# One program in two transformer blocks: a ring of twelve expert tiles, the routing block merged with the norm before it, and the output stored from the loop's block

## What is computed

```
# recurrence, per head: a 64x64 state S, one step per token
S = S * w_t + (S z_t) b_t^T + v_t k_t^T;  y_t = S r_t

# end of layer 1
xl = xl + g1 * mix_l                                # projection and residual
h  = rmsnorm(xl, norm2_g) * (1 + sc2) + sh2         # 256 tokens x 1024
logits = h @ router                                 # 256 x 8
top_logit, top_e = top_k(logits, 2); gates = softmax(top_logit)
y[t] = sum over the 2 chosen e: gates * (silu(h @ w_gate[e]) * (h @ w_up[e])) @ w_down[e]   # hidden width 3584
xl = xl + g2 * y
out = rmsnorm(xl, final_g)
```

## Time and profile before

| What | Value |
|---|---|
| Median of three runs | 3042.98 us |
| The profiled execution, its own time | 3046.43 us |
| Its span | 3044.6 us |
| Mean granted TensorE clock | 0.962 |
| PE busy | 2809.3 us (92%) |
| DVE, ACT, POOL busy | 964.3, 438.5, 175.5 us |
| First expert tile on PE | 2010.8 us |
| Expert weights, 8 items of 44 MB | 352 of the 557 MB read |

### The profile page before, as it was taken

How to read it: one execution, slowest core, us unless ns; L and a number is a source line. 1 busy time by engine, 2 the same in 40 slices (tenths; PEclk the granted TensorE clock), 3 DMA queues, 4 the chain that set the end, 5 groups by cost and what they waited for, 6 DMA issues and landing times. The chain is left out here.

```text
span 3044.6 us, 54863 instructions
## 1 busy us (share of the span) xinstructions
PE 2809.3 (92%) x24263; PEld 1632.7 (54%) x24263; DVE 964.3 (32%) x1936; ACT 438.5 (14%) x980; POOL 175.5 (6%) x210
## 2 busy tenths in 40 slices
PE   8999998699889799999979979789999999999998
PEld 6678986444478564444444457645344453434534
DVE  2422586538654326640025654320000000000001
ACT  1401100213332110000023141200000000000001
POOL 0000000000134000000000034000000000000000
PEclk9999999899999899999989989889999999999999
DMA  7234577221300125532222120069999899999995
GB/s 237 97 129 146 190 249 246 90 97 60 83 4 3 56 83 193 202 116 76 76 74 83 71 44 3 11 273 367 341 347 365 329 350 344 348 366 338 349 339 212
DMA packets 181989, 562.28 MB, mean 185 GB/s; under 512 B 28752, under 2 KB 41420, under 8 KB 165370
## 3 DMA queue, kind: packets, MB, share of 16 engines
q1 hardware_dynamic: 160675, 497.73, 45.6%
q0 software_dynamic: 13856, 53.11, 4.9%
q10 hardware_dynamic: 7223, 7.85, 0.9%
HBM read 557.43 MB, written 1.23 MB: 183 GB/s over the span
## 5 line engine op out<-in xcount | busy, mean ns | idle before, releaser
L1279 PE MATMUL bank<-normed,weight_ring 128*128 128x256 f32 (+2 forms) x2528 | 668.1, 425 | 12.7 <-PEq L2165 7.9
L1279 PEld LDWEIGHTS bank<-normed,weight_ring 128*128 128x128 f32 x2528 | 456.6, 192 | 220.7 <-issue 181.4
L2637 PE MATMUL bank<-weight_ring,work 128*32 128x384 f32 (+1 forms) x3072 | 310.7, 560 | 36.0 <-issue 34.8
L680 PE MATMUL bank<-normed,weight_ring 128*128 128x512 f32 (+1 forms) x704 | 281.6, 561 | 24.7 <-PEq L1377 24.7
L2637 PE MATMUL bank<-work 128*32 128x384 f32 (+1 forms) x3072 | 298.0, 540 | 0.0
L1279 PE MATMUL bank<-work,weight_ring 128*128 128x256 f32 (+2 forms) x928 | 282.1, 462 | 4.3 <-PEq L1247 4.3
L229 DVE SCALAR_TENSOR_TENSOR work<-work,small 128x512 f32<-128x512 f32 x336 | 237.7, 749 | 28.4 <-DMA work<-in_mod_w 21.9
L1279 PEld LDWEIGHTS bank<-work,weight_ring 128*128 128x128 f32 x928 | 174.8, 191 | 107.8 <-issue 94.2
L2637 PEld LDWEIGHTS bank<-weight_ring,work 128*32 128x32 f32 x3072 | 100.5, 113 | 235.1 <-issue 235.1
L680 PEld LDWEIGHTS bank<-normed,weight_ring 128*128 128x128 f32 x704 | 135.5, 194 | 169.7 <-issue 165.4
L2637 PEld LDWEIGHTS bank<-work 128*32 128x32 f32 x3072 | 97.4, 110 | 183.6 <-issue 183.6
(11 more groups left out here) (347 smaller groups left out, 2423.4 us busy)
## 6 DMA issues: line engine op xcount, KB each, us to landing
weight_ring<-in_moe_w_down SPq DMA_DIRECT2D x64, 1024.0 KB, 10.4
work<-in_mod_w POOLq DMA_DIRECT2D x48, 1024.0 KB, 6.1
work<-in_moe_w_down SPq DMA_DIRECT2D x48, 1024.0 KB, 10.9
weight_ring<-in_w_in SPq DMA_DIRECT2D x36, 1024.0 KB, 5.4
weight_ring<-in_moe_w_gate SPq DMA_DIRECT2D x32, 1024.0 KB, 5.5
work<-in_moe_w_gate SPq DMA_DIRECT2D x32, 1024.0 KB, 8.5
weight_ring<-in_moe_w_up SPq DMA_DIRECT2D x32, 1024.0 KB, 5.3
work<-in_moe_w_up SPq DMA_DIRECT2D x32, 1024.0 KB, 6.4
```

Source lines behind the costliest of these rows:

```text
L680: last = self.nc.tensor.matmul(self.bank(t)[:, 0:a.shape[-1]], tile[:, j * P:(j + 1) * P], a, start=k == 0, stop=k == DT - 1)
L1279: last = nc.tensor.matmul(banks(gi)[j][:, to], w[:, k, j * P:(j + 1) * P], a, start=k0 + k == 0, stop=k0 + k == total - 1)
L2637: last = nc.tensor.matmul(self.bank[3 * up + a][g * R:(g + 1) * R, 0:n], xg[:, k, a * R:(a + 1) * R], w[:, g * n:(g + 1) * n], start=k == ...
```

## The change

It has five parts.

- **Recurrence.** The product with the identity goes. The first of the two other products starts the sum. DVE now adds the old state to the sum from PSUM, in place, and then multiplies by the decay: two additions and two products instead of two products.
- **Ring of 12.** Eight slots in `work`. The first four k tiles of down come singly, in 0.5 MB tiles, so an item has 48 tiles, four turns of 12. A slot of the next item waits for the tile twelve before it.
- **Routing.** The loads go onto ACT's queue at the start of the last projection. The second half of the norm leaves that block and stands in the routing block. There PE turns the rows of token tile 0, sums the squares, computes the logits of tile 0, then those of tile 1 feature by feature behind the norm. DVE makes each tile's choice when its logits are there. The gates come behind the list of items. The first gather stands in this block as well. SP starts the first twelve tiles at its beginning, always those of expert 0; item 0 is always one of expert 0. POOL clears the buffers.
- **Residual.** DVE adds gate column times scattered rows from PSUM to the residual, eight operations of 128x256 in place of four additions of 128x512; `acc` goes, and so do the eight operations behind the loop.
- **End.** The store stands in the loop's block. The last scatter is in two halves in different banks, each followed by its own four operations on DVE; PE turns pieces of the residual as they are done; ACT loads the table of the root before the squares.

Some semaphores now share a name with others, to make room for the new ones; that adds no instruction. Cut to its core, the diff is below. Its places are, in order: the constant; `scan_pe`; `scan_dve`; `block_two` in layer 1; the routing block in `experts`; DVE in the loop's block; and PE, ACT and DVE behind the loop.

```diff
-EXPERT_SLOTS = 8
+EXPERT_SLOTS = 12
...
-            for d in range(2):
-                nc.tensor.matmul(S[d][:, 0:2 * P], self.pr.tab("ident"), self.state[:, 2 * d:2 * d + 2].rearrange("p f n -> p (f n)"),
-                                 start=True, stop=False)
-                    nc.tensor.matmul(S[d][:, fc], btok[r, 2 * d + 1, fc], self.vtok[r, tile[d], fc], start=False, stop=False)
+                    nc.tensor.matmul(S[d][:, fc], btok[r, 2 * d + 1, fc], self.vtok[r, tile[d], fc], start=f == 0, stop=False)
...
             dve.wait_ge(self.ssum.sem, self.ssum.at(n + 1))
+            for d in range(2):
+                both = self.state[:, 2 * d:2 * d + 2]
+                nc.vector.tensor_tensor(both, S[d][:, 0:2 * P].rearrange("p (f n) -> p f n", f=2), both, ALU.add).then_inc(self.carried.sem, 1)
             dve.wait_ge(self.dready.sem, self.dready.at(n + 1))
             for d in range(2):
-                last = nc.vector.tensor_tensor(self.state[:, 2 * d:2 * d + 2], S[d][:, 0:2 * P].rearrange("p (f n) -> p f n", f=2),
-                                               self.decay[:, c, 2 * d:2 * d + 2], ALU.mult)
+                both = self.state[:, 2 * d:2 * d + 2]
+                dve.wait_ge(self.carried.sem, self.carried.at(2 * n + d + 1))
+                last = nc.vector.tensor_tensor(both, both, self.decay[:, c, 2 * d:2 * d + 2], ALU.mult)
...
-                self.linear(groups, tail=norms[1])
+                final_gain = ar.take("final_gain", D)
+                route_tables, loads = self.route_loads()
+                self.linear(groups, loads=[(final_gain, bass.AP(ins["final_g_2"].tensor, 0, [[0, P], [1, D]]))] + loads)
                 ar.free("cvout")
-                final_gain = ar.take("final_gain", D)
-                self.experts(gates(1)[0][1], final_gain)
-        self.store(final_gain)
+                self.experts(gates(1)[0][1], norms[1], final_gain, *route_tables)
...
+            @block.sync
+            def _(sync):
+                for j in range(EXPERT_SLOTS):
+                    sync.dma_start(place(j), source(j, 0)).then_inc(full[j].sem, 16)
+            @block.gpsimd
+            def _(pool):
+                nc.gpsimd.memset(y[:, 1:A], 0.0).then_inc(ymoved.sem, A)
+                nc.gpsimd.memset(y[:, 0], 0.0).then_inc(added.sem, 1)
+                nc.gpsimd.memset(spread, 0.0).then_inc(gmoved.sem, 1)
             @block.tensor
             def _(pe):
+                turn_rows(0)
+                norm.add_up(pe, self.bank[3])
                 for t in range(2):
                     for k in range(DT):
+                        if t == 1:
+                            norm.wait_scaled(pe, k)
                         last = nc.tensor.matmul(self.bank[t][:, 0:E], hT[:, k, SEQ + t * P:SEQ + (t + 1) * P], router[:, k, :], start=k == 0, stop=k == DT - 1)
                     last.then_inc(logits.sem, 1)
+                turn_rows(1)
+                pe.wait_ge(choices.sem, choices.at(2))
...
+                pe.wait_ge(rowsm.sem, rowsm.at(1))
+                pe.wait_ge(picked.sem, picked.at(1))
+                gather()
             @block.scalar
             def _(act):
+                norm.square(act, lambda eng, k: None)
+                move_rows(0)
+                norm.root_and_shift(act)
+                nc.scalar.activation(gt[:, 0, 80:81], self.tab("ones")[:, 0:1], ACT.Exp)
+                move_rows(1).then_inc(rowsm.sem, 1)
 ...
+                act.wait_ge(gathered.sem, gathered.at(1))
+                move_gathered()
...
-                def add_scattered():
-                    for g in range(4):
-                        part = acc[:, 2 * g:2 * g + 2].rearrange("p k t -> p (k t)")
-                        last = nc.vector.tensor_tensor(part, self.bank[3 + g], part, ALU.add)
-                    last.then_inc(added.sem, 1)
+                def add_scattered(k, apart=False):
+                    part = self.bank[scatter_bank(k % 2, k // 2, apart)][:, (k % 2) * SEQ:(k % 2 + 1) * SEQ]
+                    return nc.vector.scalar_tensor_tensor(xT[:, k, LAT], part, gate_column(k), xT[:, k, LAT], ALU.mult, ALU.add)
...
-                scatter()
+                scatter(apart=True)
+                for k in range(DT):
+                    pe.wait_ge(added.sem, n_items + added.at(1 + max(4, k // 2 + 4 * (k % 2) + 1)))
+                    for t in range(2):
+                        last = nc.tensor.transpose(self.bank[3 + 2 * t + k // 4][:, (k % 4) * P:(k % 4 + 1) * P],
+                                                   xT[:, k, SEQ + t * P:SEQ + (t + 1) * P], ident)
+                nc.scalar.activation(stat[:, 0, 6:7], self.tab("ones")[:, 0:1], ACT.Sqrt)
+                for i, (b, t) in enumerate(((0, 0), (0, 1), (1, 0), (1, 1))):
+                    act.wait_ge(rows.sem, rows.at(i + 1))
+                    nc.scalar.activation(dump[:, 2 * t + b], self.bank[3 + 2 * t + b], ACT.Square, accum_out=stat[:, t, b:b + 1]).then_inc(squared.sem, 1)
+                for i in range(2):
+                    dve.wait_ge(scattered.sem, n_items + scattered.at(i + 1))
+                    for g in range(4):
+                        add_scattered(2 * g + i, apart=True).then_inc(added.sem, 1)
```

More of the change, by code:

```diff
@@ new lines, in experts @@
+        starts = (0, 4 * GROUP)
+        n_in, n_single = 4 * DT, 4
+        down = [(k, 1) for k in range(n_single)] + [(k, 2) for k in range(n_single, D_FFE // P, 2)]
+        per = n_in + len(down)
+        assert per % EXPERT_SLOTS == 0
+        width = 4 * GROUP
+        more = ar.take("more_slots", EXPERT_SLOTS - WEIGHT_SLOTS, width)
+        slots = [self.ring[:, i].rearrange("p k n -> p (k n)") for i in range(WEIGHT_SLOTS)] + [more[:, i] for i in range(EXPERT_SLOTS - WEIGHT_SLOTS)]
+        for i, q in enumerate(self.slot_full):
+            q.advance(16 * len(self.weights[i::WEIGHT_SLOTS]))
@@ new lines, in experts, with source @@
+        full = self.slot_full + [self.counted(f"side_load{i}_landed") for i in range(EXPERT_SLOTS - WEIGHT_SLOTS)]
+        turns = per // EXPERT_SLOTS
+        used = self.tile_used
+        wg, wu, wd = (ins[f"moe_w_{n}_2"][0] for n in ("gate", "up", "down"))
+        def source(j, e):
+            if j < n_in:
+                part, k = divmod(j, DT)
+                w, (c, n) = (wg, wu)[part % 2], (starts[part // 2], 4 * widths[part // 2])
+                return w.rearrange("e r c -> (e r) c")[bass.ds(e * D + k * P, P), c:c + n]
+            rows = wd.rearrange("e r c -> (e r) c")
+            k, n = down[j - n_in]
+            return rows[bass.ds(e * D_FFE + k * P, n * P), :].rearrange("(k p) n -> p k n", p=P)
@@ L2516, in experts @@
-        pick = ar.take("pick", 2, ITEM_TOKENS)
         gated = ar.take("gated", 2, A, P)
-        spread = ar.take("spread", A, SEQ)
-        widths = (GROUP, (D_FFE - 4 * GROUP) // 4)
-        starts = (0, 4 * GROUP)
-        n_in, n_down = 4 * DT, D_FFE // (2 * P)
-        per = n_in + n_down
-        width = 4 * GROUP
-        more = ar.take("more_slots", EXPERT_SLOTS - WEIGHT_SLOTS, width)
-        slots = [self.ring[:, i].rearrange("p k n -> p (k n)") for i in range(WEIGHT_SLOTS)] + [more[:, i] for i in range(EXPERT_SLOTS - WEIGHT_SLOTS)]
```

299 lines of the change are left out of this document (129 added, 170 removed).

## The result

The changed kernel takes 3006.71 us (median of 4 runs, 3004.55 to 3008.84). The kernel before took 3042.4 beside it (4 runs, 3039.94 to 3046.82). The ratio is 0.988, with a 95% interval of 0.9866 to 0.9894: 35.7 us less. Forecast were 3014 and a range of 3003 to 3027.

The account below looks back on a forecast made before the run. PE's own matrix work was taken to bound the loop, leaving way in, way out and recurrence: -18.5-6-4.8=-29.3 from the median 3042.98 gives 3013.7, predicted as 3014, range 3003 to 3027.

Parts of the forecast that it names:

- Ring, 0: Expert tile ring of 12: no gain, as PE was not seen to wait for any tile; 0 us.
- Way in, -18.5: Last residual to first expert tile: shorter chain, gather hidden beside DVE's list; 18.5 us less, bounds 12 to 25.5.
- the slow first tile: Loop entry: some 3 us of PE idle behind the gather slow the first tiles; 2.6 us added to the way in.
- PE doesn't catch up: First expert tiles: twelve issued early at 3 us a tile, nine there at the first tile, so PE never waits.
- Way out, -6: Last scatter's start to last scaling: the scaling starts 6.2 us earlier, counted as 6 us less; bounds 4 and 7.5.
- Recurrence, -4.8: Recurrence's 16 chunks: identity product goes, DVE gets additions; 4.8 us less, bounds -17 and +12.
- Loop, +0: Loop over items: eight DVE operations for four behind the scatter are covered, 0; without that cover 0.8 us an item.
- The edge was weights: Rival, edges between items: the ring takes perhaps 3 us off each of 7 edges, 2993 us; chance 0.06.
- Overlap pays less: Rival: instruction fetch competes with 12 MB of tiles, routing stays slow; 18 us gain in all, 3025; chance 0.15.
- Port lock: Rival, recurrence: DVE's decay product loses 0.96 us per chunk to a port shared with POOL; 3029 us; chance 0.06.
- Deeper queue, slower edge: Rival, jumps back: more tiles queue before the instruction fetch; doubled edges give +40, 3054 us; chance 0.04.
- An extra item: Rival, item list: forcing item 0 to expert 0 adds an item of 127 us, 3141, if without tokens; chance 0.01.

Follow-up runs that it names:

- both edges: Changed kernel with eight slots instead of twelve: 3006.81 us with the loop as it was, 2968.32 us with PE's back edge announced.
- the announced loop: Changed kernel with one more instruction on PE at the loop's head that announces the target of the jump back: 2967.03 us.
- -8.8 alone: Kernel before with only the recurrence's two edits, no product with the identity and two additions on DVE: 3033.11 us, ratio 0.9973.
- free queues: Changed kernel with the first twelve expert tiles started in the loop's block, after the item count is read: 3012.04 us, 5.3 more.
- before with the announcement: Kernel before with nothing but the back edge of PE's loop announced: 3014.0 us, ratio 0.9905.

## Why the prediction was right, point by point

- **Ring, 0.** Right, shown with both edges (3006.81 for 3006.71; 2968.32 for 2967.03). That the edge was the jump back and not weights is shown by the announced loop. The landing times of the tiles grew: the median of the gate tiles in `weight_ring` was 5.5 us before, 11.7 in the changed kernel with eight slots and 16.0 with twelve. With twelve more of them are under way at once, and PE waits for none of them.
- **Way in, -18.5.** It was -22.6, and +1.4 for the slow first tile: -21.2. The bounds (12 to 25.5) hold it. The chain was as described, with the gather level with DVE's list. Wrong was the logits' clock: 3.5 for each half was taken from a stretch at 0.50, though the 10 us of idle PE that had lowered it were one of the things that the change removes. The halves took 1.85 and 2.43, and the second follows ACT's shift (2.45), so 1.9 of those 7.0 us were gained and not 3.5. The entry took 1.8 behind DVE's end and not 2.5. The slow first tiles cost 1.4 and not 2.6, but this was one execution: in four others with such an entry they cost 2.9 (8.2 to 8.3 us), so the term was sound and its miss is luck. The first expert tile was forecast near 1985 and came at 1973.05; of the 12 us, 4.6 lie ahead of the first recurrence, 4.8 in the recurrence, 0.9 between and 1.6 here. (The 4.6 of gain that the prediction puts ahead of that tile should be 4.8 by its own term.) The first tile was forecast with the twelve loads running early, but their price (5.3) stood nowhere in the sum: "PE doesn't catch up" was right, and the early start was what it rested on.
- **Way out, -6.** It was -7.4, at the edge of the bounds (7.5). The same error: the 4.4 from the first transpose to the end of the squares was a time at the half clock. A square itself takes 0.60 in both kernels, but before, each waited for PE's transposes, and they followed each other every 0.85; now it is every 0.58, and the 4.4 became 3.6. Another 0.4 is that the scaling of token tile 0 starts before the root of tile 1 is taken. No drain shows behind the load of the table.
- **Recurrence, -4.8.** It was -9.6 in the profile and -8.8 alone: the term that was mis-sized most. The step that failed is "I take 0.30 for all 16". The reasoning for the one chain holds within the last step alone (-0.39 for -0.30; two additions move the decay by 0.67 and not by 0.76). Nowhere else is it 0.30: across to the last step it is -1.0, within a step -1.15, and across to a new step it lies between -0.1 and +0.8. The prediction named both ways of hiding, PE's time behind POOL and ACT and DVE's time behind an idle DVE, but put their difference at the same 0.30 without a row. And the row that it gave for DVE, the 1.52 before line 598, is not the wait that hides the additions; that is the 0.79 behind it.
- **Loop, +0.** Its edges and first tiles grew by 1.8 us over seven edges (34.8 to 35.8 in waits, 51.8 to 52.6 in the 48 instructions behind each). Nothing in the change touches them and the sum left them at 0. It is within what differs between executions: with eight slots the latter came to 51.0.
- **Rivals.** *The edge was weights*: falls, by the announced loop. *Overlap pays less*: falls, since routing took the same with free queues and with 12 MB in them. *Port lock*: falls as a cost. The product with the decay took 415 to 505 ns in all 32 instances, as this row of its line has it (min, median, max):

```profile
L600 DVE TENSOR_TENSOR work<-work x32: 415/419/505, 899.9 to 1904.6; 128x256 f32<-128x256 f32 x32
```

The order of the operations does not keep POOL out altogether. In 6 chunks an operation of POOL that reads SBUF (line 627) starts 0.03 ahead of the first product and runs beside both. The first keeps its 0.42, the second takes 0.50, and POOL's takes 0.84 where its neighbours take 0.60. SBUF — State Buffer in the Trainium skill (section SBUF: two separate sides) says that of a DVE instruction with two SBUF inputs and a GpSimd instruction that reads SBUF the one that starts first has the shared ports for the whole instruction, and the other is blocked. These rows show a contention, with POOL held by 0.24 and DVE by 0.09, and no product that waited out a whole POOL operation. It costs DVE 6x0.09=0.5 us, not 15.4. *Deeper queue, slower edge*: falls, with eight slots the edges are the same. *An extra item*: did not come, 8 items ran.

The errors of three terms point the same way: -2.7, -1.4 and -4.8, together 8.9. The loop's 1.8 goes against them, and the forecast of 3014 was 7.3 too high. That the time still lies in the range is in part luck. The low end took the recurrence at its middle, 4.8, and not at its bound of 17. With the recurrence as measured and the way in and the way out at their good bounds it would have been 3000.

## What to carry to other kernels

PE's wait for "issue" at the turn of this loop, whose body has thousands of instructions, went with the fetch of the code behind the jump. Where a trace shows such a wait, try to announce the back edge. Here it was worth 39.7 us, more than the whole change, and in the kernel before 29. Look then for the packet of code at the turn, to see whether it comes in time. When a change removes an idle stretch of PE, take the durations of what follows from a row at 2.4 GHz, not from the row that the idle stretch had slowed. Where work moves from one engine to another inside a pipelined loop, go through the kinds of chunk one by one. For each, look at the next wait of an engine behind the place of the change: a wait there can take up added time, or grow by the saved time. One average for all chunks was half of what was measured here.

## What the runs showed of the hardware

- From the landing of the 16 KB packet of instructions to PE's first instruction out of it is 1.7 to 2.0 us, at all 21 edges of three kernels (before, after, and before with the announcement); the packet itself takes about 1 us while the tiles' queue fills the DMA engines.
- The announcement doesn't always bring the packet early enough: 4.2 to 4.6 us ahead of the loop's first instruction there was no stall, at 2.8 ahead 1.1 us of it were left. In both kernels it put the packet where another had come without it. At the loop's end it cost 1.4 us in the changed kernel and nothing in the kernel before.
- An idle stretch of PE costs twice: the seven edges of about 5 us each lengthened the 48 instructions behind them from 5.36 to between 6.7 and 8.3 us, in both kernels. With edges of 1.13 us none of the seven was slow. With edges of 1.95 to 2.61 us two were, those of 2.26 and 2.43, and not the longest.
- An operation of POOL that reads SBUF took 0.84 us instead of 0.60 beside two DVE products with both operands in SBUF; the second of these took 0.50 instead of 0.42.
